# Small TensorE matmuls issued in groups of 32 or 64 stationary columns, in a kernel of two transformer blocks

## What is computed

```python
# first block: compressed keys and values (15 blocks of 32 tokens, 4 heads: 60 rows)
flat = jnp.swapaxes(blocks, 2, 3).reshape(bsz, n_cmp, ATT_KV_HEADS, CMP_BLOCK * ATT_HEAD_DIM)
return jax.nn.silu(flat @ w1) @ w2              # w1: 2048 x 256, w2: 256 x 64, for k and for v
s_cmp = jnp.einsum('bshgd,bihd->bhgsi', q_grp, k_cmp).astype(jnp.float32) * scale
# first block: SSD inside a chunk of 128 tokens, 16 heads of 64
y_diag = jnp.einsum('bclsgh,bcsghp->bclghp', cb[..., None] * decay, x)
# second block: recurrence inside a chunk
rel = jnp.where(tri[:, :, None], cum[:, :, :, None, :] - cum[:, :, None, :, :], -jnp.inf)
scores = jnp.einsum('bhtk,bhsk,bhtsk->bhts', qc, kc, jnp.exp(rel))
```

## Time and profile before

| | before |
|---|---|
| median of 3 runs | 2498.62 us (2496.06 to 2498.85) |
| the profiled execution, its own time | 2493.09 us |
| span of the profiled execution | 2491.3 us |
| PE busy | 2459.0 us, 99% |
| weight loads (PEld) busy | 2083.2 us, 84% |
| DVE, ACT, POOL busy | 60%, 50%, 2% |
| mean of the 16 DMA engines, busy | q1 56.2% |

### The profile page before, as it was taken

The page is one execution under the profiler, slowest core; times in us unless marked ns, Lnnn a source line. Parts: engine busy times, 40 slices in busy tenths (PEclk is TensorE's granted clock), DMA queues, the critical chain, the costliest instruction groups (busy, mean ns, idle before and its releaser), DMA issues.

```text
span 2491.3 us, 33794 instructions
## 1 busy us (share of the span) xinstructions
PE 2459.0 (99%) x12543; PEld 2083.2 (84%) x12543; DVE 1490.7 (60%) x1754; ACT 1256.5 (50%) x1605; POOL 44.9 (2%) x103
## 2 busy tenths in 40 slices
PE   8999999999999999999999999999999999999997
PEld 7888878888888888888888888888888888888886
DVE  5478765545445454445656656557777777644465
ACT  4357744444444444444654345456656556444464
POOL 2300000000000000000000000000000000000000
PEclk9999999999999999999999999999999999999999
DMA  7553445666666666556564555555556556655554
GB/s 250 173 144 107 134 144 186 187 192 190 188 187 189 189 193 204 190 190 186 162 180 142 148 148 175 188 152 186 186 186 198 188 185 190 208 197 193 194 194 141
DMA packets 234755, 446.29 MB, mean 179 GB/s; under 512 B 14288, under 2 KB 31012, under 8 KB 234144
## 3 DMA queue, kind: packets, MB, share of 16 engines
q1 hardware_dynamic: 231920, 434.83, 56.2%
q0 software_dynamic: 2736, 10.10, 1.4%
HBM read 442.78 MB, written 2.10 MB: 179 GB/s over the span
## 4 chain that ended last, share of the span: by engine, by line
PE 96%; DVE 2%; ACT 1%; issue 0%; DMA 0%; SPq 0%; DVEq 0%; ACTq 0%
PE pg L2209 20%; PE pg L2211 20%; PE pg L2210 20%; PE pt L2685 6%; PE pg L2685 6%; PE pt L2689 3%; PE pg L2689 3%; PE pg L2268 3%; PE pg L2269 3%; PE pg L2270 3%; PE pt L2889 1%; PE pt L2280 1%; DVE wlo L1353 1%; PE pt L2388 1%; PE pt L2453 1%; PE pt L2479 1%
## 5 line engine op out<-in xcount | busy, mean ns | idle before, releaser
L1353 DVE TENSOR_TENSOR wlo<-raw,whi 128x1024 fp32r<-128x1024 f32 (+3 forms) x844 | 1003.3, 1196 | 917.3 <-ACT whi L655 915.7
L655 ACT ACTIVATE whi<-raw 128x1024 fp32r<-128x1024 f32 (+3 forms) x844 | 871.4, 1036 | 1143.5 <-PE pg L2211 843.1
L2209 PE MATMUL pg<-whi,A 128*128 128x512 f32 (+1 forms) x1216 | 471.9, 388 | 4.2 <-DVE A L1492 3.1
L2211 PE MATMUL pg<-whi,A 128*128 128x512 f32 (+1 forms) x1216 | 467.8, 385 | 0.0
L2210 PE MATMUL pg<-wlo,A 128*128 128x512 f32 (+1 forms) x1216 | 467.3, 384 | 0.0
L2209 PE MATMUL pg<-whi,FH 128*128 128x512 f32 x696 | 271.3, 390 | 0.0
L2211 PE MATMUL pg<-whi,FL 128*128 128x512 f32 x696 | 270.9, 389 | 0.0
L2210 PE MATMUL pg<-wlo,FH 128*128 128x512 f32 x696 | 270.9, 389 | 0.0
L2209 PEld LDWEIGHTS pg<-whi,A 128*128 128x128 f32 x1216 | 229.0, 188 | 48.9 <-DVE A L1492 3.5
L2211 PEld LDWEIGHTS pg<-whi,A 128*128 128x128 f32 x1216 | 228.9, 188 | 45.7
L2210 PEld LDWEIGHTS pg<-wlo,A 128*128 128x128 f32 x1216 | 229.1, 188 | 43.7
(11 more groups left out here) (494 smaller groups left out, 2765.5 us busy)
## 6 DMA issues: line engine op xcount, KB each, us to landing
raw<-w_up SPq DMA_DIRECT2D x264, 512.0 KB, 3.8
raw<-w_down SPq DMA_DIRECT2D x176, 512.0 KB, 3.6
raw<-w_in SPq DMA_DIRECT2D x152, 512.0 KB, 3.6
raw<-w_gate SPq DMA_DIRECT2D x88, 512.0 KB, 3.6
raw<-w_out SPq DMA_DIRECT2D x64, 512.0 KB, 3.6
raw<-w_ple_gate SPq DMA_DIRECT2D x32, 512.0 KB, 3.8
raw<-w_in SPq DMA_DIRECT2D x32, 388.0 KB, 3.2
raw<-w_in SPq DMA_DIRECT2D x16, 280.0 KB, 3.0
```

What stands on the lines that cost most here:

```text
L655: A(whi[:, n % RING, 0:w], raw[:, n % RING, 0:w], ACT.Copy).then_inc(hi_ready, 1)
L1353: V.tensor_tensor(wlo[:, n % RING, 0:w], raw[:, n % RING, 0:w], whi[:, n % RING, 0:w].bitcast(F32), ALU.subtract).then_inc(lo_ready, 1)
L2209: mm(o, xh, wh, start=first and k == 0, stop=False)
L2211: ins = mm(o, xl, wh, start=False, stop=last and k == SK - 1)
```

## The change

The matmuls named above are cut along their stationary columns into groups of 32 or 64, each of which writes to its own 32 or 64 output partitions. `hidden` computes keys and values in one go at step 29, the keys' 60 columns in the lower half of the output partitions and the values' in the upper half, in turn. `lv_diagonal` and the levels compute only the blocks on the diagonal that lie in each group of columns. The output places and what reads them change only for `hidden` (`HT_` is now [128, 256]; `hid_silu` has two instructions for one).

```diff
+            def by_columns(size, o, lhs, rhs, start=True, stop=True):
+                for c in range(0, P, size):
+                    ins = mm(o[c:c + size], lhs[:, c:c + size], rhs, start=start, stop=stop)
+                return ins
...
-            def hidden(i):
-                if i == 0:
-                    pe.wait_ge(cmpw_landed, 16 * 11)
-                    pe.wait_ge(q_out, 2)
-                w, x = ((W1K, KFK), (W1V, KFV))[i]
+            def hidden():
+
+                pe.wait_ge(cmpw_landed, 16 * 11)
+                pe.wait_ge(q_out, 2)
                 for k in range(KT):
-                    ins = mm(pt[0:60, 0, i * CMP_HID:(i + 1) * CMP_HID], x[:, k, :], w[:, k, :], start=k == 0, stop=k == KT - 1)
+                    mm(pt[0:60, 0, 0:CMP_HID], KFK[:, k, :], W1K[:, k, :], start=k == 0, stop=k == KT - 1)
+                    ins = mm(pt[64:124, 0, 0:CMP_HID], KFV[:, k, :], W1V[:, k, :], start=k == 0, stop=k == KT - 1)
...
-                        ins = mm(dst[:, c0:c0 + 32], q[:, x, t * P:(t + 1) * P], KCB[:, 2 * i + x // 2, :], start=True, stop=True)
+                        ins = by_columns(32, dst[:, c0:c0 + 32], q[:, x, t * P:(t + 1) * P], KCB[:, 2 * i + x // 2, :])
...
-                    ins = mm(pt[:, h // 8, (h % 8) * HD:(h % 8 + 1) * HD], M[:, t, h, :], XD[:, t, h * HD:(h + 1) * HD],
-                             start=True, stop=True)
+                    ins = by_columns(64, pt[:, h // 8, (h % 8) * HD:(h % 8 + 1) * HD], M[:, t, h, :], XD[:, t, h * HD:(h + 1) * HD])
...
-                if n in (28, 29):
-                    hidden(n - 28)
+                if n == 29:
+                    hidden()
...
-                        ins = mm(head_place(t, h), HKT[:, t, h * P:(h + 1) * P], HQ[:, t, h * P:(h + 1) * P], start=True, stop=True)
+                        k, q = HKT[:, t, h * P:(h + 1) * P], HQ[:, t, h * P:(h + 1) * P]
+                        for m in range(4):
+                            r = slice(32 * m, 32 * m + 32)
+                            ins = mm(head_place(t, h)[r, r], k[:, r], q[:, r], start=True, stop=True)
...
+                elif l <= 2:
+                    b = LEVELS[l - 1]
...
+                            for m in range(64 // b):
+                                k0 = 2 * b * m
+                                ins = mm(o[k0:k0 + b, b * m:b * (m + 1)], g[:, k0:k0 + b], g[:, k0 + b:k0 + 2 * b],
+                                         start=True, stop=True)
                 else:
                     b = LEVELS[l - 1]
                     for t in range(NT):
                         for h in range(8):
                             g = LG[l % 2][:, t, h * P:(h + 1) * P]
-                            ins = mm(pt[:, lv_bank(l) + t, h * 64:(h + 1) * 64], g, g.rearrange("p (m a b) -> p m a b", a=2, b=b)[:, :, 1, :],
-                                     start=True, stop=True)
+                            q = g.rearrange("p (m a b) -> p m a b", a=2, b=b)[:, :, 1, :]
+                            o = pt[:, lv_bank(l) + t, h * 64:(h + 1) * 64]
+                            for m in range(4):
+                                r = slice(32 * m, 32 * m + 32)
+                                ins = mm(o[r, 16 * m:16 * m + 16], g[:, r], q[:, 16 * m // b:16 * (m + 1) // b, :], start=True, stop=True)
```

More of the change, by code:

```diff
@@ L255, in two_blocks @@
         ZX = at("ZX", [P, NT, 4 * W_XB], F32, o_x)
-        HT_ = at("HT_", [P, 2 * CMP_HID], F32, o_x)
+        HT_ = at("HT_", [P, CMP_HID], F32, o_x)
         RT = at("RT", [P, 4, NT, 8, ROPE_HALF], F32, o_x + 2048)
@@ L819, in hid_silu @@
                 act.wait_ge(hid_sum, 1)
-                A(HT_[0:60, :], pt[0:60, 0, :], ACT.Silu).then_inc(hid_act, 1)
+                A(HT_[0:60, :], pt[0:60, 0, 0:CMP_HID], ACT.Silu)
+                A(HT_[64:124, :], pt[64:124, 0, 0:CMP_HID], ACT.Silu).then_inc(hid_act, 1)
             def hid_out():
                 act.wait_ge(hid_turned, 1)
-                hid = pt[:, 1, 0:256].rearrange("p (b c) -> p b c", c=64)
-                A(HK[:], hid[:, 0:2, 0:60], ACT.Copy).then_inc(hid_act, 1)
+                hid_k, hid_v = (pt[:, b, 0:P].rearrange("p (m c) -> p m c", c=64) for b in (1, 0))
+                A(HK[:], hid_k[:, :, 0:60], ACT.Copy).then_inc(hid_act, 1)
                 act.wait_ge(zeroed, 2)
@@ L828, in hid_out @@
                     for h in range(NKV):
-                        x = hid[:, 2 + m, h * NCMP:(h + 1) * NCMP].unsqueeze(1).to_broadcast([P, 4, NCMP])
+                        x = hid_v[:, m, h * NCMP:(h + 1) * NCMP].unsqueeze(1).to_broadcast([P, 4, NCMP])
                         ins = A(HV[:, m, h, :, 0:NCMP], x, ACT.Copy)
@@ L2380, in k_turn @@
                 ins.then_inc(k_turned, 1)
-            def hidden(i):
-                if i == 0:
-                    pe.wait_ge(cmpw_landed, 16 * 11)
-                    pe.wait_ge(q_out, 2)
-                w, x = ((W1K, KFK), (W1V, KFV))[i]
+            def hidden():
+                pe.wait_ge(cmpw_landed, 16 * 11)
+                pe.wait_ge(q_out, 2)
                 for k in range(KT):
-                    ins = mm(pt[0:60, 0, i * CMP_HID:(i + 1) * CMP_HID], x[:, k, :], w[:, k, :], start=k == 0, stop=k == KT - 1)
-                if i:
-                    ins.then_inc(hid_sum, 1)
+                    mm(pt[0:60, 0, 0:CMP_HID], KFK[:, k, :], W1K[:, k, :], start=k == 0, stop=k == KT - 1)
+                    ins = mm(pt[64:124, 0, 0:CMP_HID], KFV[:, k, :], W1V[:, k, :], start=k == 0, stop=k == KT - 1)
+                ins.then_inc(hid_sum, 1)
             def hid_turn():
@@ L2394, in hid_turn @@
                 for i in range(4):
-                    ins = tr(pt[:, 1, i * 64:i * 64 + 60], HT_[0:60, i * P:(i + 1) * P], C[0:60, 0:60])
+                    r = slice(64 * (i // 2), 64 * (i // 2) + 60)
+                    ins = tr(pt[:, 1 - i // 2, (i % 2) * 64:(i % 2) * 64 + 60], HT_[r, (i % 2) * P:(i % 2 + 1) * P], C[r, r])
                 ins.then_inc(hid_turned, 1)
@@ L2401, in cmp @@
                 for m in range(2):
-                    mm(pt[:, 1, 256:316], W2K[:, m].rearrange("p a d -> p (a d)"), HK[:, m, :], start=m == 0, stop=m == 1)
+                    by_columns(64, pt[:, 1, 256:316], W2K[:, m].rearrange("p a d -> p (a d)"), HK[:, m, :], start=m == 0, stop=m == 1)
                 for h in range(NKV):
                     for m in range(2):
-                        ins = mm(pt[:, 2, h * HD:(h + 1) * HD], HV[:, m, h].rearrange("p g i -> p (g i)"), W2V[:, m, :],
-                                 start=m == 0, stop=m == 1)
+                        ins = by_columns(64, pt[:, 2, h * HD:(h + 1) * HD], HV[:, m, h].rearrange("p g i -> p (g i)"), W2V[:, m, :],
+                                         start=m == 0, stop=m == 1)
                 ins.then_inc(cmp_sum, 1)
@@ L2883, in lv_level @@
                         ins = mm(head_place(0, h), LG[0][:, 0, h * P:(h + 1) * P], LG[0][:, 1, h * P:(h + 1) * P], start=True, stop=True)
+                elif l <= 2:
+                    b = LEVELS[l - 1]
+                    for t in range(NT):
+                        for h in range(8):
+                            g = LG[l % 2][:, t, h * P:(h + 1) * P]
+                            o = pt[:, lv_bank(l) + t, h * 64:(h + 1) * 64]
[3 more added lines that the diff above has]
+                                         start=True, stop=True)
                 else:
```

## The result

The changed kernel takes 2462.68 us (median of 4 runs, 2462.32 to 2462.89), the kernel before on the same chips 2497.34 us (4 runs, 2495.94 to 2498.85); the ratio is 0.9861, 95% interval 0.9844 to 0.9878. From profiled execution to profiled execution it is 2493.09 to 2462.56 us, 30.5 us less. So the sum over the parts was right to 0.7 us, and what it was taken off was not.

What follows compares the result with a forecast made beforehand. PE, busy 99%, was taken as the bound, its side groups by weight loads. Savings of 15.6 + 4.3 + 1.9 + 0.8 + 7.2 = 29.8 us off the 2498.62 us median gave 2468.8 us, range 2465 to 2483.

Steps and rivals of the forecast that it cites:

- the sum over the parts: Savings of all cut groups on PE: 15.6 + 4.3 + 1.9 + 0.8 + 7.2 = 29.8 us.
- The bound, and the pace of a pass: PE's side groups before: bound by weight loads of 128 columns, 0.112 us a pass, 3.57 us for 32 passes.
- The slots: Time in which each column group does one pass: 0.031 us with 32 columns, 0.056 us with 64.
- The entry of 0.35: Cost on PE of entering and leaving each group of side work: 0.09 + 0.05 + 0.10 + 0.11 = 0.35 us.
- "Does it arrive?": Levels' chain through ACT and DVE keeps some 0.4 us slack; level 2's 1.41 us wait for DVE stays, so savings arrive.
- A slot of 32 as long as one of 64: Rival in the 32-column groups: 256 slots each 0.025 us longer, 6.4 us of gain lost, 2475.2 us; chance 0.10.
- One pass in 28 or 55 ns at best: Two rivals on PE's start rate whatever the groups: 28 ns gives 2487.8 us, chance 0.07; 55 ns 2517.7, slower, 0.04.
- the Trainium skill's floor of 25 ns: Opposing rule on matmul starts, however few columns move: four groups need 100 ns a slot, some 17 us of gain lost.
- what the Trainium skill says of small moving dimensions: Opposing rule: one moving column takes as long as 60, so 16 and 32 would be no cheaper than 64.
- Late work: Rival at levels 3 to 7: DVE or weights come no sooner, 11.2 us lost, 2480 us; chance 0.08.
- instruction fetch: Rival: seven groups each wait once for instructions, 3.6 us, 25 us in all, 2494 us; fetch or dearer entry 0.05.
- "The forecast goes by the median: 2498.62 - 29.8": Final step: the saving taken off the three-run median, 5.5 us above the profiled 2493.09 us, giving 2468.8 us.

Runs made afterwards that it cites:

- e12: Changed kernel with 64 moving columns in place of 16 in levels 3 to 7: 2466.44 us, four runs, 2466.2 to 2466.8.
- e8: Changed kernel with the matmuls of levels 3 to 7 and the recurrence's diagonal issued group by group, not in turn: 2478.66 us, four runs.
- e9: Changed kernel with level 2 alone put back as before (128 stationary, 64 moving columns): four runs, 2465.6, 2467.7, 2467.9, 2468.8 us.
- e11: Kernel before with only level 2 in groups of 32 and diagonal(1) in groups of 64: median 2488.79 us, eight runs, 2486.9 to 2489.1.
- e13: Kernel before with only level 2 in groups of 32: eleven runs, seven from 2489.4 to 2491.8 us, four from 2493.7 to 2494.0.
- e10: Changed kernel with diagonal(1) alone put back as before: four runs, 2463.4 to 2464.1 us.
- e3: Kernel before with only cs, the recurrence's diagonal and levels 2 to 7 in groups of 32: median 2475.01 us, five runs, 2473.8 to 2475.4.
- e1: Kernel before, run again without an edit: median 2495.96 us, eleven runs, 2492.91 to 2498.99.
- e2: Kernel before with only the edit of hidden: five runs, 2485.1, 2485.2, 2485.4, 2488.3, 2491.2 us.
- e14: Kernel before with only diagonal(1) in groups of 64: eleven runs, eight from 2490.1 to 2490.9 us, three from 2495.4 to 2496.2.
- e6: Kernel before with level 2 and diagonal(1) each moved one step later: eleven runs, all from 2490.7 to 2491.9 us.

## Why the prediction missed, step by step

- **The bound, and the pace of a pass** (weight loads of 128 columns, 0.112 us): right. A quarter of the columns is a load 83 ns shorter, 84 by the step of 28.
- **The slots.** 0.031 us taken, 0.033 measured. The entry of 0.35 is the one measured on L2479 before; the length of one group gives only the sum of entry and slots. Each part by the same measure, forecast and found: the recurrence's diagonal 1.34 and 1.44, level 2 1.34 and 1.42, level 3 1.34 and 1.40, `hidden` 7.25 and 7.25. So the cut groups cost up to 0.1 us more each than forecast. But 3.57 us before was low for some: levels 4, 6 and 7 had cost 3.83 to 3.86 (level 4 from 1353.67 to 1357.96 us, less 0.45), and level 2 3.84 behind its wait. All parts measured in this way save 30.3 us; the sum was 29.8 us, the profiles give 30.5.
- **"Does it arrive?"**: right. Level 2's wait is 1.41 us as before, and no new one of that size came. One reading under it was wrong: the clock of the kernel before was not at full in every slice, the page's row of nines only hides 6.8 us at half near 1640 us. Since the changed kernel has them too, the sum did not suffer.
- **The rivals.** A slot of 32 as long as one of 64: wrong for 16 moving columns (0.033), right as soon as 64 move (0.056, e12). One pass in 28 or 55 ns at best: wrong across groups (8 ns), right within one (29 ns, e8). By the Trainium skill's floor of 25 ns ("TensorE: Matmul & The Clock Gate", Part 1) level 3 would take over 3.2 us; it takes 1.40, so the floor does not hold across groups (the 17 us that the prediction put on it add up to 16), while e8's 29 ns within one group don't contradict it. By what the Trainium skill says of small moving dimensions ("TensorEngine Tiling (Array Packing)", Performance Considerations) 16 columns would take as long as 60; e12 against the changed kernel gives 1.7 times as long a slot for 64 as for 16, so it doesn't hold here either. Late work and instruction fetch: neither shows (PE's waits after are those of before to 0.2 us each); fetch was not tested by itself.
- **The step that failed: "The forecast goes by the median: 2498.62 - 29.8".** The 5.5 us between the profiled execution and the median were carried over as if every kernel had them. They were no constant: they were in the main time at a clock of 1.2 GHz that some executions have at level 2 and `diagonal(1)`, and that no run of the changed kernel shows. The profiled execution had neither; like the changed kernel's it had only the 6.8 us that the earlier trace rows hide. From it, 2493.09 - 29.8 = 2463.3, within 0.6 us of the 2462.68 measured. What ended the fall at level 2 is a shorter group behind the same wait, not a shorter wait (e9, e11); that the same holds at `diagonal(1)` rests on four runs in eleven of e13 against none in eight of e11. There was bad luck in it too: the base, a median of three, was one of the longest lengths, and the medians of before in the later batches were 2494.9 to 2495.7. From 2495.7 the same sum gives 2465.9, inside the range, with the same step wrong.

What is left open: why the clock falls in some executions and not in others of the same kernel, and why the stretch near 1640 us has different lengths. And whether `diagonal(1)` at full length would fall in the changed kernel too: e10's four runs without it, when e13 had seven of eleven without, don't decide that. In e3 it did not fall in five runs with that group untouched, which may be chance as well.

## What to carry to other kernels

Where float32 matmuls with few moving columns stand at 0.11 us a pass, count stationary columns: cut into groups of 32 or 64 that write to different partitions, and issue them in turn, not group by group. Where only part of the product is used, as here, cut the moving columns too: with 64 of them the slot was 0.056 us and not 0.033. The price is about 0.35 us (from L2479) each time the array goes from whole to groups and back, so as an estimate it pays from some five passes of 128 columns on, cut into four groups of 32 (5 x 0.112 minus 5 x 0.033 is 0.40).

A spread of lengths in one kernel is a finding, not noise to take a median over. When the timed runs lie away from the profiled one, forecast each length for itself, and look for a place where PE idles and a group of low pace follows. Look in windows of a few us; the page's row of 40 slices showed none of these falls.

## What the runs showed of the hardware that was not expected

- TensorE's granted clock fell to 1.2 GHz for 6.8 to 10.2 us behind an idle of only 0.8 to 1.4 us, in a kernel in which PE is 99% busy, when 32 passes of 0.112 us came behind it: 1 to 2.7 us after they began (e1, e2, e9, e14). By the run times it cost some 3 to 5.5 us each time. With cut groups behind the same idle (1.2 us at level 2, 2.1 at `diagonal(1)`), or with the big stream behind it or no idle at all, the longer lengths did not appear, in the eight runs of the changed kernel and the eleven of e6.
- Around two waits of PE of 3.2 and 1 us, in the second block, it was at 1.2 GHz in each of the sixteen profiled executions, for 3.4, 6.8 or 10.2 us.
- 128 passes of 32 columns, 256 instructions of weight loads and matmuls, go through in 1.27 us, about one in 5 ns.
